# Neighbourhood attention on one core: VectorE's copy of a turned part set ahead of the next maximum, and the context's maximum by a plain reduce

## The reference, cut to what matters

```python
s_nb = jnp.einsum('brqhd,brkwhd->bhrqkw', qg, k_blk).astype(jnp.float32) * scale
s_nb = s_nb + bias.astype(jnp.float32)[None]
s_nb = jnp.where(in_win[:, None, :], s_nb, -jnp.inf)
s_cx = jnp.einsum('brqhd,bchd->bhrqc', qg, k_ctx).astype(jnp.float32) * scale
sc = jnp.concatenate([s_nb.reshape(b, h, rows, GRID_W, n_nb), s_cx], axis=-1)
p = jax.nn.softmax(sc, axis=-1).astype(v.dtype)
```

## Time and profile before

| | us |
|---|---|
| runs: median (lowest to highest) of 3 | 4208.19 (4207.66 to 4209.45) |
| the profiled execution: its own time | 4207.78 |
| its span in the trace | 4205.9 |
| neighbourhood's heads, layer 0, first and last start of line 2480 | 2730.2 to 2906.5 |
| neighbourhood's heads, layer 1, the same | 3913.8 to 4062.6 |

### The profile page before, as it was taken

The page is one execution under the profiler, slowest core; times in us unless marked ns, Lnnn a source line. Parts: engine busy times, 40 slices in busy tenths (PEclk is TensorE's granted clock), DMA queues, the critical chain, the costliest instruction groups (busy, mean ns, idle before and its releaser), DMA issues. The chain is left out here.

```text
span 4205.9 us, 69100 instructions
## 1 busy us (share of the span) xinstructions
PE 3618.9 (86%) x24826; PEld 2974.0 (71%) x24826; DVE 2489.0 (59%) x4501; ACT 2047.6 (49%) x3639; POOL 815.8 (19%) x504
## 2 busy tenths in 40 slices
PE   4988699987579999669998899975989998899759
PEld 4984587776458888558886677754768786788647
DVE  2205365533678887547753777755647745877655
ACT  2216456741057777443223666654433325666542
POOL 1213100020036666323330000002023430000020
PEclk7998899998689999879998999997989999999989
DMA  7226733413969999633235434241233327244413
GB/s 271 87 99 210 201 80 81 81 44 132 348 253 394 395 396 394 227 122 108 84 102 155 116 62 99 55 99 56 78 134 113 108 86 202 46 93 93 92 50 97
DMA packets 410473, 624.68 MB, mean 149 GB/s; under 512 B 103596, under 2 KB 266164, under 8 KB 409108
## 3 DMA queue, kind: packets, MB, share of 16 engines
q1 hardware_dynamic: 395472, 566.58, 43.4%
q0 software_dynamic: 10976, 40.51, 3.0%
q10 hardware_dynamic: 3684, 13.17, 1.0%
HBM read 486.19 MB, written 133.97 MB: 147 GB/s over the span
## 5 line engine op out<-in xcount | busy, mean ns | idle before, releaser
L1362 ACT ACTIVATE aa_prob<-aa_ps,aa_nm 128x256 f32<-128x256 f32 (+2 forms) x680 | 474.2, 697 | 273.1 <-DVEq L1313 235.3
L1233 PE MATMUL aa_ps<-aa_op 128*128 128x512 f32 (+2 forms) x1408 | 376.7, 381 | 171.0 <-DVEq L1321 127.4
L1312 DVE TENSOR_REDUCE aa_nm<-aa_ps 128x1 f32<-128x1280 f32 (+1 forms) x252 | 346.1, 1373 | 219.7 <-PE aa_ps L1233 207.4
L1233 PEld LDWEIGHTS aa_ps<-aa_op 128*128 128x128 f32 x1408 | 236.4, 194 | 293.7 <-issue 161.7
L2091 PE MATMUL pr_ps<-pr_wH,hT_part 128*128 128x512 f32 (+1 forms) x1120 | 432.9, 387 | 0.0
L1856 ACT ACTIVATE ex_high<-ex_ring 128x2048 fp32r<-128x2048 f32 x192 | 368.7, 1920 | 97.9 <-PE ex_pg L1832 40.1
L1902 DVE TENSOR_TENSOR ex_ring_part<-ex_ring,ex_high 128x2048 fp32r<-128x2048 f32 x144 | 370.0, 2570 | 50.9 <-ACTq L1857 39.6
L1263 PE MATMUL aa_po<-aa_pT,aa_op 128*64 128x128 f32 x5552 | 392.9, 284 | 0.0
L2091 PE MATMUL pr_ps<-pr_wH,x_sb_part 128*128 128x512 f32 x896 | 366.3, 409 | 13.8 <-POOL pr_ws_part L2241 7.0
L1244 PE MATMUL aa_ps<-ident,aa_prob 128*128 128x128 f32 x2776 | 374.0, 278 | 2.6 <-ACTq L1366 2.6
L2091 PE MATMUL pr_ps<-pr_ws_part,x_sb_part 128*128 128x512 f32 x896 | 356.4, 398 | 0.0
(11 more groups left out here) (315 smaller groups left out, 7015.4 us busy)
## 6 DMA issues: line engine op xcount, KB each, us to landing
ex_ring<-in_w_gate SPq DMA_DIRECT2D x64, 1024.0 KB, 9.7
ex_ring<-in_w_up SPq DMA_DIRECT2D x64, 1024.0 KB, 8.1
ex_ring<-in_w_down SPq DMA_DIRECT2D x64, 1024.0 KB, 7.9
aa_op<-z_d SPq DMA_DIRECT2D x120, 320.0 KB, 8.3
z_d<-pr_zT SPq DMA_DIRECT2D x120, 256.0 KB, 2.8
pr_ws<-in_w_in SPq DMA_DIRECT2D x12, 2048.0 KB, 8.3
mod_w<-in_w_ada SPq DMA_DIRECT2D x10, 2048.0 KB, 13.4
rt_mw<-in_w_ada SPq DMA_DIRECT2D x8, 2048.0 KB, 14.5
```

Of the source, the lines that this page charges most:

```text
L1233: mm = tensor.matmul(ps[:, base[h] + at:base[h] + at + m], q.bitcast(F32R), kk.bitcast(F32R), start=i == 0, stop=i == len(ab) - 1)
L1312: vector.tensor_reduce(most, scores[:, 0:g_.count[t]], AX.X, ALU.max, negate=True)
L1362: scalar.activation(prob[:, base[h] + c0:base[h] + c1], ps[:, base[h] + c0:base[h] + c1], ACT.Exp, bias=nm[:, h % 4:h % 4 + 1], scale=-1.0 ...
```

## The change

Two edits, both in neighbourhood's heads. First, DVE's order within a slot: `turned_part(s-2)` is called ahead of `maximum(s)` where step s and all steps turned in the slot belong to this group; elsewhere the order stays. The waits inside both are the same. Second, the context's 256 columns are reduced by a `tensor_reduce` with a negated maximum in place of the `tensor_tensor_reduce`; they stay in PSUM as they are, so the exponential over them has scale 1 and the one over the neighbours keeps -1. The buffer `zeros` and its filling go.

```diff
@@ class Heads
+        def sign(self, t, x):
+
+            return -1.0 if self.add_bias is not None and (not self.apart or (x == 0 and len(self.spans[t]) == 2)) else 1.0
+
@@ stage_attention, vector block, loop over the slots
                     for m in tiles_at(s, 5):
                         finished(m)
+
+                    first = s < n and steps[s][0].apart and all(steps[g][0].apart for g in turning(s))
+                    for g in turning(s) if first else ():
+                        turned_part(g)
                     if s < n:
                         maximum(s)
-                    for g in turning(s):
+                    for g in () if first else turning(s):
                         turned_part(g)
@@ stage_attention, scalar block, exponentials
                                               bias=nm[:, h % 4:h % 4 + 1],
-                                              scale=-1.0 if g_.add_bias is not None else 1.0,
+                                              scale=g_.sign(t, x),
                                               accum_out=den[:, m % RING, x, j:j + 1])
@@ second_layer
             def last_edge(dve):
                 vector.tensor_tensor(G[:, :, NEARK + 2 * P:], G[:, :, 0:2 * P], edge, ALU.add)
-                vector.memset(zeros[:, :], 0.0)
                 dve.drain()
...
             def bias(dve, scores, most, p, j, t):
                 c0, c1 = (512, 512 + CTX) if t < ST else (0, CTX)
-                vector.tensor_tensor_reduce(scores[:, c0:c1], scores[:, c0:c1], zeros[:, :], -1.0,
-                                            3e38, ALU.add, ALU.min, least[:, :] if t < ST else most)
+
+                vector.tensor_reduce(least[:, :] if t < ST else most, scores[:, c0:c1], AX.X, ALU.max, negate=True)
...
-            G, mask, zeros, least = (held.enter_context(nc.sbuf_tensor(f"{x}{l}", shape, F32)) for x, shape in (
-                ("G", [P, HC, NEARB]), ("nearm", [P, 1, NEARK + 2 * P]), ("zeros", [P, CTX]), ("least", [P, 1])))
+            G, mask, least = (held.enter_context(nc.sbuf_tensor(f"{x}{l}", shape, F32)) for x, shape in (
+                ("G", [P, HC, NEARB]), ("nearm", [P, 1, NEARK + 2 * P]), ("least", [P, 1])))
```

## The result

The kernel after takes **4226.94 us** (median of 5 runs, 4217.81 to 4232.91), the kernel before, on the same chip, 4208.19 (5 runs, 4206.06 to 4210.61): a ratio of **1.0047** (95% interval 1.0036 to 1.0059), 19 us slower. The longer executions have no trace; their mean granted clock over the whole program is 0.927 to 0.930, against 0.931 in the profiled one.

What follows compares the result with a forecast made beforehand. Bound: a ring of waits through DVE's maximum and copy, 6.28 us a pair of steps. Terms +0.5 - 0.4 - 3.8 - 1.0 + 2.0 = -2.7 on 4207.8 give 4205.1, as a median 4205.5 us; range 4188 to 4215.

Steps and rivals of the forecast that it cites:

- What bounds the kernel: Neighbourhood's heads: a ring of waits between PE and DVE, through DVE's maximum and copy, 6.28 us a pair of steps.
- the new ring: Neighbourhood's heads: waits through PE, DVE, ACT and PE, closed at `turned`; nine links, 6.29 us a pair, +0.5 us in all.
- The uneven steps: Layer 1: the two steps of a pair take about 2.0 and 4.2 us, where before has 3.02 and 3.26.
- The first rival: Neighbourhood's heads: the path closes by ACT's own copy, not through `turned`; 5.94 us a pair, 4189 us; chance 0.30.
- From the copy to the reduce: DVE's idle time between its copy of the turned part and the reduce: 0.27 us, bounds 0.11 and 0.42.
- The reduce: DVE's context maximum by a plain reduce: next operation starts after 0.54 us instead of 0.61, 0.07 less a step.
- Off the path: DVE's `finished` leaves the ring; a cover of 1.05 us hides its addition lengthened during POOL's weight splitting: -3.8 us, eight pairs.
- The terms of -0.4 and -1.0: -0.4 us for the two dropped fillings of `zeros`; -1.0 us for the context's own steps and each group's first steps.
- Where PE is slow: Layer 0 at PE's lower clock: a pair takes 7.8 us instead of 7.2; +2 us taken.
- six pairs of layer 0: Two slow-clock pairs behind each start of a pair of heads in layer 0, costing 0.6 us each: +3.6 us.
- The second rival: Neighbourhood's heads: PE's single pause of some 1.9 us lowers its clock, pairs of 7.8 us, slower, up to 4241; chance 0.14.
- the eight-pair case: Eight more pairs of layer 1 at PE's lower clock, 1.5 us each over today's, make the kernel slower by over 0.2%.

Runs made afterwards that it cites:

- run 4: Kernel after with ACT's `values_out` one slot earlier, behind its copy and ahead of the odd slot's exponentials: 4168.55 us, ratio 0.9904.
- run 8: Kernel after without the `ticks` increment between DVE's copy and the reduce: 4192.52 us with ten identity transposes ahead of `turned` (first kernel), 4212.49 us without transposes.
- run 1: Kernel after with DVE's old order restored, keeping the plain reduce: 4194.96 us, ratio 0.9965.
- run 3: Kernel after with ten identity transposes on PE ahead of its wait at `turned`, in even slots of neighbourhood's heads: 4200.17 us, ratio 0.9976.
- run 10: The kernel of run 9 with the small two-input addition of `finished` replaced by a one-input reduce: 4151.24 us, ratio 0.9864.
- run 6: Kernel after with DVE's old order restored, the plain reduce kept, and `values_out` one slot earlier: 4190.73 us, ratio 0.9967.
- run 9: Kernel after with `values_out` one slot earlier and no `ticks` increment behind DVE's copy, no transposes added: 4161.70 us, ratio 0.9887.

## Why the prediction was wrong

**What bounds the kernel, and the new ring: right.** Each link can be laid beside the timeline of after. Forecast 0.67, 0.75, 0.69, 0.54, 0.75, 1.49, 0.35, 0.24 and 0.81, measured 0.69, 0.74, 0.66, 0.54, 0.75, 1.50, 0.35, 0.26 and 0.81, sum 6.30; the pairs are 6.29. The uneven steps, PE's wait at `turned` for ACT and the end of the wait for L1325 are as said. The first rival (5.94, closed by ACT's copy) did not occur; that it is a real ring is seen in run 4, where it binds at 5.40, shorter because `values_out` is off it.

**From the copy to the reduce: 0.27 forecast, 0.24 measured**, and run 8 explains it: half of it is the increment of `ticks`. The Trainium skill (VectorE: DVE Perf Modes, The DRAIN you can't avoid) has a semaphore cost nothing extra, measured there on eight copies with a semaphore after each. Here an increment that is an instruction of its own between two operations costs 0.12. The measurement decides.

**The reduce: 0.07 a step forecast, 0.10 measured** (run 1). The Trainium skill's warning against `tensor_reduce` (same page, Rules for kernel authors) doesn't hold against the operation that it replaces here: 425 ns against 433 and a second instruction of 141.

**"Off the path", -3.8 us: right in kind, too large.** I had the small addition stay at 0.72, fully hidden by a cover of 1.05. But its length is not its own. It ends with whatever POOL instruction it has met, and the new ring meets other ones. In run 3, where the clock is out of the way, the excess over its usual 0.16 is 0.72, 1.35 and 1.68 in layer 1, and the pairs are 6.29, 6.53 and 6.86: longer by what exceeds 1.11. Layer 1 lost 0.8 by it in that run and layer 0 0.55 (pairs of 6.62 and 6.51), so of before's 0.5 x 8 some 2.6 were gained, by estimate. The terms of -0.4 and -1.0 no run isolates.

**"Where PE is slow", +2 us: this is the step that failed.** Its price for a pair was right: "the new one holds scores, transposes and value products: 7.8"; measured 7.83 to 7.86 for the longest pairs, 7.60 for that of the timeline above. What was wrong is the number of pairs. I took the clock "as it is" and gave it six pairs of layer 0. In fact five steps of layer 1 and eight of layer 0 are longer than 5 us in the profiled execution, where before has none, and others are lengthened in part. Three things led there:

- I had the cause in hand ("the new ring lets PE pause once, some 1.9 us long, where it now pauses twice") and treated it as a rival with a condition, 0.14, since the clock was 1.00 in layer 1. That row tells of a PE that pauses for 1.3 us in an ordinary pair and never for more than 1.64, and says nothing of one of 1.9.
- I read one low window of layer 0. Before was below 0.95 in 10 of the 18 windows there already, mean 0.87: not an exception behind the context's tiles but more than half of the stretch. The clock did stay "as it is" there (0.87 and 0.88), and layer 0 grew by 8.0 all the same. In time, 46 us at the lower level is indeed about six pairs of 7.2. But the slow time doesn't come in whole pairs. The window from 4010 to 4020 is at the lower level for a part of its length only (0.83). That part holds value products, scores and transposes, which is nearly all of PE's work on the ring, and the step takes 5.73 where the same step takes 4.18 in run 3: the 1.5 that I asked for a wholly slow pair. The runs give the price of a slow microsecond, by estimate: in the new order, after against run 3, 14.1 us for 31 us in layer 0 (0.46 each) and 5.8 for 21 in layer 1 (0.27); in the old order, before against run 1 in layer 0, 4.9 for 33 (0.15). My pairs come to 1.5 / 7.8 = 0.19 and 0.9 / 7.2 = 0.13.
- I looked at how busy PE is. After, it is busy for 75.4 us of 103.4 where it was 68.9, and the clock is lower; part of the 75.4 is work that takes longer at the lower level. Pair for pair at the upper level the total of the pauses didn't change (run 3); their shape did.

The second rival was the true case, with its mechanism and its price for a pair as written. Its place only in part: it counted pairs of layer 1, and 8.0 of the 10.8 us fell in layer 0. Its first condition, two more pairs of layer 1 to cancel the gain, was met and passed. The Trainium skill (TensorE: Matmul & The Clock Gate, A second HAM failure mode: psum-queue depth-cycling) describes a picture like this one, and the trace of after agrees: windows of 1.00 and 0.83 by turns. With the clock held up the kernel takes 4200 (run 3), within the forecast range; with the clock up in layer 0 too, as it mostly is in that run, my own sum is 4205.5 - 2 - 5.4 = 4198. The range's upper end was made of six slow pairs; the eight-pair case and beyond, which I had worked out, lay outside, and that is where it came out.

**The sign of it** was named: "a granted clock under 1.00 in 3926 to 4029". It is 0.95.

## What to carry to other kernels

When an edit merges two short pauses of PE into one long one, price the ring at both clock levels and ask how near the stretch already is to the fall, from every window of every layer and not from the best one. A few transposes of the identity ahead of the wait tell in one run whether the clock or the ring is the loss (4227 to 4200 here). And when a ring is cut, look in each engine's queue for the small work that the cut leaves behind something long: one ACT operation of 0.28 us, moved one slot in the new order, was worth 58 us, where the change by itself had cost 19.

## What the runs showed of the hardware

- **Where PE's one pause was longer, the clock fell more often.** In pairs of about 6.2 to 6.3 us, the kernels with a pause of 1.93, 1.82 and 1.71 ahead of the turn had 21, 19 and 13 windows below 0.95, those with 1.49, 0.85 and 0.72 four or less. The transposes add work too (ten are busy for 1.25 us), so that the rows with them alone don't part pause from work. After and the kernel without the increment have none: 21 of 36 and 19 of 35 with one long pause in pairs of 6.29 and 6.17, against 13 of 34 in before (pairs of 6.28) and 6 of 32 in run 1 (6.08) with two short ones. In run 10 PE is busy for 95.8 us of the 120 from 3890 to 4010, and every window there has 1.00. These are readings of this kernel's rows, of one profiled execution each, and give no rule.
- **Executions of one kernel scatter, in part ahead of what the edits touch.** After's five runs span 15 us, the eleven with two transposes 14 and the eleven with four 14 as well, though the traces of these two have 13 and four low windows; the six with ten and no increment span 3. The first reduce of neighbourhood's heads in layer 0 starts anywhere from 2728.6 (after) to 2739.5 us (run 6) in the traces, so some 11 us of difference come ahead of the stretches compared here. What makes them is open.
- **The small DVE addition with two SBUF inputs is held until the POOL instruction in progress ends.** In before, after and runs 3, 4 and 9 every lengthened addition, 0.22 to 1.97 us, ends within 0.03 us of the end of the POOL instruction that was running when it started; with one input, none is lengthened. The Trainium skill (SBUF — State Buffer, SBUF: two separate sides) states this lock of the shared ports for a DVE operation with two SBUF inputs, and the runs agree. The lock also drew some pairs of run 9 to 6.86, which is two of POOL's rounds of 3.43.
- **An increment of a semaphore as an instruction of its own costs DVE 0.12 us**, and it counts once for each time that it lies on the ring: 0.12 x 48 is 5.8 of the 8 us between run 3 and the first kernel of run 8.
